# The factors of a chunked recurrence are formed beside it instead of in a stage of their own

## The reference

```
for d in range(2):
    w_log = -softplus(-(w0[d] + tanh(u @ w1[d]) @ w2[d])) - 0.5
    decay = exp(-exp(w_log))
    a = sigmoid(a0[d] + (u @ a1[d]) @ a2[d])
    kd = k * (1 + (a - 1) * k_a)
    y += wkv7_scan(r, decay, kd, v, kk, a, reverse=(d == 1))
    bonus += sum(r * kd * r_k) * v

# one step of wkv7_scan, state of 64x64 per head:
state = state * w_t - (state @ kk_t) (kk_t * a_t)^T + v_t k_t^T
y_t   = state @ r_t
```

## Time and profile before

| | us |
|---|---|
| median of 3 runs | 3428.79 (3424.62 to 3430.26) |
| profiled execution, its own time | 3421.95 |
| its span, first to last instruction | 3419.8 |
| preparation | 664.4 to 863.3 |
| start of the recurrence, until PE's first transpose | 863.3 to 872.4 |
| eight pairs | 872.4 to 1321.5 |
| finish | 1322.8 to 1370.6 |
| busy: PE, DVE, ACT, POOL | 2876.0, 1434.9, 961.4, 757.6 |

### The profile page before, as it was taken

How to read it: one execution, slowest core, us unless ns; L and a number is a source line. 1 busy time by engine, 2 the same in 40 slices (tenths; PEclk the granted TensorE clock), 3 DMA queues, 4 the chain that set the end, 5 groups by cost and what they waited for, 6 DMA issues and landing times. The chain is left out here.

```text
span 3419.8 us, 56487 instructions
## 1 busy us (share of the span) xinstructions
PE 2876.0 (84%) x24048; PEld 2333.8 (68%) x24048; DVE 1434.9 (42%) x1990; ACT 961.4 (28%) x1316; POOL 757.6 (22%) x358
## 2 busy tenths in 40 slices
PE   2798979634799997488999999964979799999997
PEld 1576757311798985367888888853867688888885
DVE  5464655178333344163333333343215333343345
ACT  2211235234223232232222132134224313212222
POOL 1311110034000001413233233214131323222321
PEclk8899989766899998698999999986979899999999
DMA  4546650243301100413121111022021311111113
GB/s 150 192 153 231 219 162 21 82 131 107 122 34 65 35 34 21 147 68 92 37 61 49 37 58 47 24 73 89 1 87 68 96 40 49 51 47 43 55 31 111
DMA packets 250766, 275.33 MB, mean 81 GB/s; under 512 B 27987, under 2 KB 192047, under 8 KB 248539
## 3 DMA queue, kind: packets, MB, share of 16 engines
q1 hardware_dynamic: 240940, 266.35, 24.3%
q10 hardware_dynamic: 9648, 6.34, 0.6%
HBM read 218.08 MB, written 54.58 MB: 80 GB/s over the span
## 5 line engine op out<-in xcount | busy, mean ns | idle before, releaser
L304 PE MATMUL cg_ps_u<-m_hi,cg_u_hi 128*128 128x512 f32 x1408 | 549.8, 390 | 29.4 <-POOL cg_u_lo L2100 29.4
L305 PE MATMUL cg_ps_u<-m_lo,cg_u_hi 128*128 128x512 f32 x1408 | 549.3, 390 | 0.0
L306 PE MATMUL cg_ps_u<-m_hi,cg_u_lo 128*128 128x512 f32 x1408 | 549.2, 390 | 0.0
L2139 DVE SCALAR_TENSOR_TENSOR cg_z<-cg_ps_u,top_conv_f,cg_z 128x1023 f32<-128x1023 f32 x88 | 112.9, 1283 | 734.2 <-ACT cg_z L2054 734.2
L2100 POOL TENSOR_TENSOR cg_u_lo<-cg_u_raw,cg_u_hi 128x1024 fp32r<-128x1024 f32 x88 | 211.2, 2400 | 695.4 <-ACT cg_u_hi L2043 695.4
L2054 ACT ACTIVATE cg_z<-cg_ps_u,top_conv_f 128x1024 f32<-128x1024 f32 x88 | 98.3, 1117 | 941.8 <-PE cg_ps_u L306 941.8
L304 PEld LDWEIGHTS cg_ps_u<-m_hi,cg_u_hi 128*128 128x128 f32 x1408 | 265.3, 188 | 85.4 <-POOL cg_u_lo L2100 30.2
L305 PEld LDWEIGHTS cg_ps_u<-m_lo,cg_u_hi 128*128 128x128 f32 x1408 | 265.3, 188 | 55.2
L306 PEld LDWEIGHTS cg_ps_u<-m_hi,cg_u_lo 128*128 128x128 f32 x1408 | 265.2, 188 | 55.3
L304 PE MATMUL cg_ps_d<-cg_d_hi,cg_a_hi 128*128 128x512 f32 x704 | 280.3, 398 | 19.3 <-issue 17.3
L2155 DVE TENSOR_TENSOR y_y<-cg_ps_d,y_y 128x512 f32<-128x512 f32 x320 | 215.4, 688 | 152.4 <-PE cg_ps_d L306 152.4
(11 more groups left out here) (345 smaller groups left out, 5135.0 us busy)
## 6 DMA issues: line engine op xcount, KB each, us to landing
cg_u_raw<-in_ffn_up SPq DMA_DIRECT2D x88, 512.0 KB, 4.0
za_mw<-in_ada_w SPq DMA_DIRECT2D x12, 2048.0 KB
cg_d_raw<-in_ffn_down SPq DMA_DIRECT2D x44, 512.0 KB
qkv_mw<-in_ada_w SPq DMA_DIRECT2D x8, 2048.0 KB
rw_st<-scr_st SPq DMA_DIRECT2D x16, 1024.0 KB
mod_w<-in_ada_w SPq DMA_DIRECT2D x8, 1024.0 KB
za_w_raw<-in_mix_in SPq DMA_DIRECT2D x16, 512.0 KB, 4.3
scr_z<-za_z SPq DMA_DIRECT2D x16, 512.0 KB
```

The lines of the kernel that those rows point to most:

```text
L304: nc.tensor.matmul(out, a_hi, b_hi, start=first, stop=False)
L305: nc.tensor.matmul(out, a_hi, b_lo, start=False, stop=False)
L306: return nc.tensor.matmul(out, a_lo, b_hi, start=False, stop=last)
L2139: V.scalar_tensor_tensor(z[:, j, 1:S], ps_u[:, j % 2, 0:S - 1], conv_cols[:, 0, bass.ds(tile_of(g, j), 1)], z[:, j, 1:S], ALU.mult, ALU.ad ...
```

## The change

The preparation no longer makes factors. It stores what they are made of: the sigmoid of the decay (lw) and of the rate (aa) for both directions, the unit keys (kk), the bonus and the gate, and the reversed values. It keeps all four feature tiles in SBUF at once, sums the squares of all heads into one tile of 4 x 32 rows, so that there is one root and one reciprocal, and makes the sum of both directions' kd from the sum of both rates. PE's result ring has three places.

The recurrence loads lw, aa, k, kk and r of a pair in its direction (ten loads of 256 KB a pair) and forms the factors of pair m + 1 while pair m is at its levels: the products all on DVE, the exponentials and the scaled rate on ACT, nothing on POOL. Before pair 0 they are formed with nothing beside them. DVE's work is dealt out to ten slots (`beside`), ACT's to three places. Bonus and gate are loaded in the finish.

```diff
 # prepare_recurrence, cut to its core
+    r, k, v = (s.sb(n, [P, KU, S]) for n in ("r", "k", "v"))
+    pb = s.ps("pb", [P, 3, S])
 # SP
+            for f in range(KU):
+                for i, dst in enumerate((lw_d[0], aa_d[0], lw_d[1], aa_d[1])):
+                    sp.wait_ge(act_read, f * NA + i + 1)
+                    sp.dma_start(dst[f], out[:, place(f, i), :]).then_inc(out_stored[place(f, i)], 16)
+                sp.wait_ge(act_read, f * NA + NA)
+                sp.dma_start(gate_d[f], gate[:, f % 2, :]).then_inc(gate_stored[f % 2], 16)
+                sp.wait_ge(vr_done, f + 1)
+                sp.dma_start(vr_d[f], vr[:, f % 2, :]).then_inc(vr_stored[f % 2], 16)
 # PE
+                for i, (lhs, rhs) in enumerate(((w2s[d0, cols], tw[d0]), (a2s[d0, cols], ta[d0]), (w2s[d1, cols], tw[d1]),
+                                                (a2s[d1, cols], ta[d1]), (g2s[:, cols], tg))):
+                    n = f * NA + i
+                    if n >= 3:
+                        pe.wait_ge(act_read, n - 2)
+                    product(n, lhs, rhs)
...
+                    ins = mm(ps_sq[32 * f:32 * f + 32, span], pick[:, :], sq[:, f % 2, span], start=True, stop=True)
...
+                if j < KU:
+                    pe.wait_ge(root_done, 1)
+                    product(n, spread[32 * f:32 * f + 32, :], root[32 * f:32 * f + 32, :])
+                else:
+                    pe.wait_ge(bonus_in, f + 1)
+                    product(n, heads[:, :], r[:, f, :])
 # ACT, behind its last feature tile
+            A(root[:, :], ps_sq[:, :], ACT.Sqrt, bias=eps[:, 0:1]).then_inc(root_in, 1)
+            rate(KU - 1)
 # DVE
+            for f in range(KU):
+                dve.wait_ge(rated_k, f + 1)
+                dve.wait_ge(rv_loaded[f], 32)
+                V.scalar_tensor_tensor(r[:, f, :], r[:, f, :], vec[:, R_K, f:f + 1], both[:, f % 2, :], ALU.mult, ALU.mult).then_inc(bonus_in, 1)
+            dve.wait_ge(root_in, 1)
+            V.reciprocal(root[:, :], root[:, :]).then_inc(root_done, 1)
+            for j in range(2 * KU):
...
+                    V.tensor_tensor(kk[:, f, :], kk[:, f, :], result(KU * NA + j), ALU.mult).then_inc(dve_read, 1)
...
+                    V.tensor_tensor(bon[:, f % 2, :], result(KU * NA + j), v[:, f, :], ALU.mult).then_inc(dve_read, 1)
 # recurrence, SP
+                    if m:
+                        sp.wait_ge(f_alpha[g], m)
+                        sp.wait_ge(f_nbeta[g], m)
+                        sp.wait_ge(f_kd[g], m)
+                        sp.wait_ge(f_rho[g], m)
+                    span = tokens_of(g, m)
+                    for dst, src in ((lw, lw_d[g]), (aa, aa_d[g]), (kx, z_d[KU:2 * KU]), (kk, kk_d), (rx, z_d[0:KU])):
+                        sp.dma_start(dst[g][:, :, :], src[:, :, span].rearrange("f p t -> p f t")).then_inc(f_loaded[g], 16)
-                    sp.dma_start(st[b][g][:, :, :], st_d[g, m]).then_inc(staged[b][g], 16)
 # ACT
+            def f_rates(g, m):
...
+                for f in range(KU):
+                    ins = A(kd[g][:, f, :], aa[g][:, f, :], ACT.Identity, scale=vec[:, K_A, f:f + 1], bias=rest_ka[:, f:f + 1])
+                ins.then_inc(f_rate[g], 1)
+            def f_exps(g, m):
+                act.wait_ge(f_centred[g], m + 1)
...
+                A(emid[g][:, :, :], mids[g][:, :, :], ACT.Exp, scale=DECAY)
+                A(e1[g][:, :, :], cc[g][:, :, :], ACT.Exp, scale=DECAY).then_inc(f_exp[g], 1)
+                act.wait_ge(f_before[g], m + 1)
+                A(lw[g][:, :, :], lw[g][:, :, :], ACT.Exp, scale=DECAY).then_inc(f_exp[g], 1)
+                A(cc[g][:, :, :], cc[g][:, :, :], ACT.Exp, scale=-DECAY).then_inc(f_exp[g], 1)
...
                 for i in range(NL):
                     for g in range(2):
                         level_u(g, m, i)
+                    if m + 1 < NPAIR:
+                        if i == 0:
+                            for g in range(2):
+                                f_rates(g, m + 1)
+                        elif i <= 2:
+                            f_exps(i - 1, m + 1)
 # DVE; f_rated, f_keys, f_rhos, f_kappas, f_nbetas are one product of 128x512 each
+            def f_scan(g, m):
+                dve.wait_ge(f_loaded[g], 80 * (m + 1))
...
+                V.tensor_tensor_scan(c[:, o], reset_row[:, :], w[:, o], 0.0, ALU.mult, ALU.add).then_inc(f_scanned[g], 1)
+            def beside(m, slot):
+                order = (((f_scan, 0),), ((f_scan, 1),), ((f_centre, 0), (f_keys, 0)), ((f_centre, 1), (f_keys, 1)), ((f_shift, 0),),
+                         ((f_shift, 1), (f_rated, 0)), ((f_rated, 1), (f_alphas, 0)), ((f_rhos, 0), (f_alphas, 1)),
+                         ((f_rhos, 1), (f_kappas, 0), (f_nbetas, 0)), ((f_kappas, 1), (f_nbetas, 1)))
...
+            for step in (f_scan, f_centre, f_shift, f_keys, f_rated, f_alphas, f_rhos, f_kappas, f_nbetas):
+                for g in range(2):
+                    step(g, 0)
...
+                beside(m, 0)
                 for i in range(NL):
                     for g in range(2):
                         level_x(g, m, i)
+                    beside(m, 2 * i + 1)
                     if i < NL - 1:
                         for g in range(2):
                             level_t(g, m, i)
+                        beside(m, 2 * i + 2)
 # finish_recurrence, SP
+            sp.dma_start(bon[:, :, :], bon_d.rearrange("f p t -> p f t")).then_inc(bon_loaded, 16)
+            sp.dma_start(gate[:, :, :], gate_d.rearrange("f p t -> p f t")).then_inc(gate_loaded, 16)
```

More of the change, by code:

```diff
@@ L947, with prepare_recurrence @@
 LEVELS = (2, 4, 8, 16, 32)
-def prepare_recurrence(nc, z_d, w2, a2, g2, consts, tw, ta, tg, ff, bon, gate, st_d, vr_d):
+def prepare_recurrence(nc, z_d, w2, a2, g2, tab, consts, tw, ta, tg, lw_d, aa_d, kk_d, bon_d, gate_d, vr_d):
     vec, heads = consts["vec"], consts["heads"]
     W0, A0, K_K, K_A, R_K = 0, 2, 4, 5, 6
-    LORA_D0, RATE_D0, SQUARES, LORA_D1, RATE_D1, GATE, BONUS = range(7)
-    NP = 7
-    ROUNDS = KU // 2
+    NA, NST = 5, 8
     with ExitStack() as ctx:
         s = Scope(nc, ctx, "rp")
[L961 to L983, removed]
-        block = s.block()
[L986 to L997, removed]
@@ new lines, in prepare_recurrence @@
+        r, k, v = (s.sb(n, [P, KU, S]) for n in ("r", "k", "v"))
+        kk = s.sb("kk", [P, KU, S])
+        w2s, a2s, g2s = (s.sb(n, [P, WA]) for n in ("w2s", "a2s", "g2s"))
+        out = s.sb("out", [P, NST, S])
+        sq, vr, gate, both, bon = (s.sb(n, [P, 2, S]) for n in ("sq", "vr", "gate", "both", "bon"))
+        root = s.sb("root", [P, S])
+        pick, spread = s.sb("pick", [P, 32]), s.sb("spread", [P, P])
+        rest, eps = s.sb("rest", [P, KU]), s.sb("eps", [P, 1])
+        pb = s.ps("pb", [P, 3, S])
@@ L999, in _, with result, place @@
+        block = s.block()
+        def result(n):
+            return pb[:, n % 3, :]
+        def place(f, i):
+            return (4 * f + i) % NST
         @block.sync
         def _(sp):
[L1001 to L1026, removed]
@@ new lines, in key, with rate @@
+            def key(f):
+                act.wait_ge(k_loaded[f], 16)
+                A(kk[:, f, :], k[:, f, :], ACT.Copy, scale=vec[:, K_K, f:f + 1]).then_inc(kk_in, 1)
+                act.wait_ge(kk_in, f + 1)
+                if f >= 2:
+                    act.wait_ge(sq_mm, f - 1)
+                A(sq[:, f % 2, :], kk[:, f, :], ACT.Square).then_inc(sq_done, 1)
+            def rate(f):
+                act.wait_ge(asum, f + 1)
+                act.wait_ge(rest_set, 1)
+                A(both[:, f % 2, :], both[:, f % 2, :], ACT.Identity, scale=vec[:, K_A, f:f + 1], bias=rest[:, f:f + 1]).then_inc(rated, 1)
@@ L1198, in recurrence @@
+def recurrence(nc, z_d, vr_d, lw_d, aa_d, kk_d, tab, consts, ff, ysum):
     ident = consts["ident"]
@@ L2394 @@
     "z": (4 * WA // P, P, S),
-    "st": (2, NPAIR, P, KU, 4 * P),
+    "lw": (2, KU, P, S),
+    "aa": (2, KU, P, S),
+    "kk": (KU, P, S),
+    "bon": (KU, P, S),
+    "gate": (KU, P, S),
     "vr": (KU, P, S),
```

352 lines of the change are left out of this document (200 added, 152 removed).

## The result

The changed kernel takes 3466.68 us (median of 4 runs, 3464.18 to 3468.46) against 3426.70 us of the kernel before in the same measurement (4 runs, 3421.66 to 3430.26). The ratio is 1.0117, 95% interval 1.0100 to 1.0135: **1.2% slower**, where 3362 us and a range of 3335 to 3400 were forecast. The profiled execution took 3464.18 us, span 3462.3.

What follows compares the result with a forecast made beforehand. It took the preparation as bound by a serial mix on DVE and its stores, the recurrence by PE; preparation -101, recurrence start +17 and pairs +17 gave -67 us, so 3362 us against 3428.79, range 3335 to 3400.

Steps and rivals of the forecast that it cites:

- rival 2: Recurrence pairs: the clock falls behind PE's waits at levels 0 and 1, costing 17 us, total 3379; chance 0.08.
- Preparation: Stage before the recurrence: shortened to 97.3 us by dropping the factors, a gain of 101 us.
- PE's 52 us for the four tiles: Preparation: six products per feature tile, 19 us at the low clock, then 18 products at 1.85 us.
- The chain behind the last product: Preparation: ACT's last passes, table load, root, rate, products and reciprocal with nothing beside them, 15.6 us.
- The eight products: Preparation: PE's products that wait for the reciprocal and start cold, taken at 18 us.
- rival 1: Preparation: the clock stays at 1.2 GHz throughout, costing 29 us, total 3391; chance 0.17.
- The DMA bound: Preparation: 23.9 MB at 273 GB/s need 88 us, so the stage cannot be shorter than 90 us.
- Start of the recurrence: Before pair 0: loads and factors with nothing beside them take 26 us, 17 us more than before.
- Slots: DVE's ten places for the next pair's factors in each pair: 2.35 us exposed a pair, 17 us over seven.
- slot 8: Late place in DVE's order in a pair: its 1.85 us of work exceeds DVE's idle 1.44, exposing 0.2 us.
- Rival 3: Recurrence pairs: slots or loads cost 6 us a pair, 42 instead of 17 us, total 3387; chance 0.15.
- Rival 4: Recurrence: DVE becomes the bound, all 12.9 us a pair on PE's path, total 3435; chance 0.05.

Runs made afterwards that it cites:

- e1: Changed kernel with DVE's steps dealt out anew: nothing ahead of level 0's copies, keys' products a level behind their scaled copies; 3324.63 us, 0.9706 of the kernel before.
- e7: Changed kernel plus 12 unread 128x128 products on PE in its wait at level 1, in seven pairs; 3366.36 us, 0.9832 of the kernel before.

## Why the prediction was wrong

**The step that failed** is in rival 2: "Against: gaps of 1.1 us leave it at 1.00", and its price, "If each pair fell for 5 us of PE time, as at the cold start ... 2.5 us x 7 = 17". The mechanism was named, the place and length of the waits were nearly right, but it got a chance of 0.08 and a seventh of its price, and the sum has no term for the clock in the pairs at all. Measured: 16.4 us of clock in a pair, 115 us in seven.

Both halves could have been read from the trace of the kernel before. The gap's effect was read from pair 2 alone. The next pair of the same trace shows a fall behind the same wait of 1.09 us (stretches view):

```profile
1057.00:1059.00 2.00, 1.53 (x37) 1.56 (x39) 0.90 (x2) 0.00 (x0) 0.00 (x0) 0.76 0.00 0
1059.00:1061.00 2.00, 2.00 (x44) 2.00 (x42) 0.69 (x1) 0.25 (x1) 0.00 (x0) 0.50 0.04 8
1061.00:1063.00 2.00, 2.00 (x68) 2.00 (x65) 0.69 (x1) 0.34 (x1) 0.00 (x0) 0.89 0.00 0
```

The mean of 0.98 in the earlier trace rows had such falls in it (three pairs of eight stand at 0.97, and the first at 0.96 for its cold start), and I took it for "no fall". For the price I took the length of the fall from the cold start, where transposes and score products of 64 and 128 columns follow. Behind level 1 come some 19 us of narrow products instead, 33 at the low clock. That a fully busy PE can stay at 0.51 was in the earlier trace rows too: I used it for the preparation and not here.

The Trainium skill's page "TensorE: Matmul & The Clock Gate", section "HAM oscillation — how this bites in real kernels", which the prediction named for this rival, describes a loop whose wait comes round each turn and finds PE cold each turn. The changed kernel agrees, seven pairs of seven. The waits in its example are for transfers, about 3 to 5 us long, and it makes such lengths the condition, so its rule taken strictly would not have foretold this fall, as the prediction said it did. Here 1.54 us did it each time and 0.56 us three times in seven, and the measurement decides.

**Point by point.**
- Preparation: forecast 97.3 us, measured 91.3 (-107.6 instead of -101). The term that was too large is PE's 52 us for the four tiles: they took 42.7 (673.3 to 716.0), for two reasons. The clock was at 1.00 from about 681 us on, 8 us behind PE's start, where I had taken 19 us at the low level. And two of a tile's six products, over different halves of the rows, ran side by side, eight records in the 1.83 us of four (688.12 to 689.95). The first two of the eight:

```profile
688.12 0.59 PE L1026 MATMUL rp_pb<-lh_ta,rp_a2s 64*128 64x512 f32 x1
688.13 0.69 PE L1026 MATMUL rp_pb<-lh_tw,rp_w2s 64*128 64x512 f32 x1
```

- The rest of the preparation: PE started 2 us later than forecast. The chain behind the last product was right: from the root's start (718.6 us) to the product that waits for the reciprocal (731.2) 12.6 us, against 12.3 of the terms behind the table load. The eight products took 18.8 us (731.2 to 750.0) against 18. The clock did not stay low, so rival 1 did not come. The DMA bound was too careful: from 678 to 712 us the queue moved 410 GB/s, not 273, with PE busy for 32.5 of these 34 us.
- Start of the recurrence: forecast 26 us, measured 24.2. Right.
- Slots: level 0's wait grew by 1.13 us (forecast 1.15), level 1's came to 1.54 (forecast 1.0). The difference is ACT: eight scaled copies of 128 columns took 3.17 us, 0.40 us each, where I had estimated 0.9 us for four; it is a size, not a mechanism. Slots 3 to 9, the loads and the finish are hidden, as forecast (slot 8 was to cost 0.2): PE's other waits for an engine come to 17.2 us in the eight pairs against 16.5, since one wait for ACT, 0.64 us before, takes 0.9 to 1.0 us in five pairs. The finish takes 46 us. Rival 3 (6 us a pair from slots and loads) fell.
- Rival 4, the only one on the slower side, was the wrong mechanism: DVE is busy for 34 of 74 us in a pair and bounds nothing. e1 has the same work and is 3% faster than before.
- Take the clock out of the account (115 us, seven times the second pair's 16.4), and the change is 42.5 - 115 = -72 us, near the -67 of the forecast. e1 shows what it is worth with both waits gone: -101 us.

## What to carry to other kernels

Price a new wait of PE by what PE does behind it, not by its length alone: ahead of level 0's products of 64 columns, waits of 1.1 to 2.2 us cost themselves and at most 7 us of low clock; ahead of a long run of products of 32 columns, waits of 0.9 to 1.5 us halved the speed of nearly everything up to the solve's products of 128, in 39 of 41 pairs. When work is dealt out beside a PE-bound loop, put nothing ahead of PE's narrow stretch, check that no step there waits for a second engine, and if a gap can't be avoided, try filling it with products that nobody reads (e7). And look at the granted clock of every turn of a loop, in stretches of 2 us, before calling it steady: a mean of 0.98 was a loop whose clock already fell now and then.
